# An HGRN2 and forgetting-attention step: a new order at the beginning, in the last recurrent head and in attention's first and last steps

## The chip, the cores and the metric

The kernel runs on one core of a Trainium2 chip, as one program. The metric is the time of one execution on the device in microseconds (us), the median of several; less is better. The engines are TensorE (PE, with PEld for its weight loads), VectorE (DVE), ScalarE (ACT), GpSimd (POOL) and SyncE (SP), whose queue issues most transfers.

## The reference

One inference step of a decoder with two layers, over 512 prompt tokens (one sequence) and 64 sample tokens (eight sequences of eight), model width 1024. In short:

```python
x = concat(x_prompt, x_sample)                 # 576 rows of 1024
h = rmsnorm(x, a_norm) @ a_w_in                # q, forget, value, gate: 8 heads of 128 each
f = lb + (1 - lb) * sigmoid(fz); k = (1 - lb) * sigmoid(-fz)
S_t = diag(f_t) S_(t-1) + k_t v_t^T; o_t = S_t^T q_t       # per head; samples start at state_hgrn
x += (rmsnorm(o, o_g) * silu(gate)) @ a_w_out
x += ffn(x)                                    # SwiGLU, 2816 wide
k, v, logf = shared_kv(x)                      # 16 heads of 64; k normed per head
q = rmsnorm(rmsnorm(x) @ b_wq)
# logit = q.k/8 + cq[t] - ck[s], causal; the samples also see 2048 past rows
# each, read from pages of 128 rows by page_table
x += softmax(logit) @ v @ b_wo
x += ffn(x)
```

Outputs are x, the recurrent states and the new k, v and logf rows.

## The kernel before, in words

Products keep the precision of float32 by splitting both sides into a rounded high part (fp32r) and the rest, the low part: high*high, high*low and low*high are summed, three matmuls for one. So each weight tile (a "unit": 128 output columns) goes SP load, ScalarE high part, GpSimd low part, then 48 matmuls of 128x288 (8 row tiles, 3 products, 2 halves of the 576 tokens). The order of the work is written out by hand for each engine; semaphores join the five lists. There are four blocks with a barrier between them.

*The first block* (`hgrn_layer`) begins with `FirstNorm`: five tiles of tokens (rows 0 to 3 of 128, row 4 of 64) are loaded, squared with a sum (L182), turned to 1/rms by one Ln and one Exp over all (L185 to L189), scaled (L169 on ScalarE, L239 on DVE), transposed by TensorE (L214), and split into xh (L196) and xl (L244). Then come eight heads of four units (q, forget, value, gate; L391). A unit's result is in PSUM banks 0 and 1, and the next unit waits until ScalarE has evicted it (`evicted`). Between the units of head h stand `scores`, `states`, `outputs` and `means` of the heads before. The last head has nothing to stand between: TensorE runs scores(7), means(6), states(7), outputs(7), and the first products of the next block. SP stores the results of head 6 before it fetches head 7's state (`fetch_state`, L343).

*The first trunk* (`trunk`, "t0") is the output product, the feed-forward and the units for q, k and v. Towards its end SP loads the first four cache pages.

*Attention* runs in steps. Steps 0 to 63 (KSTEPS = 64) each transpose two key pages (L1261; `key`), copy them out (L1420, L1551), score them (L1275), and from step 10 on mix two value pages (L1325). Every fourth group adds a decay row through `rowsel` (L1282), which is rounded from `sel`, loaded at the block's start. Eight steps are one sequence: then `exponentials` (a small one of the new rows, L1436, then two halves, L1438), `probabilities` (L1307) and, after the last page, eight matmuls with the new values, `vn` and `ptt` of 8 partitions (L1331). Between, the prompt's own attention is done in 32 pairs of units (L1358 to L1379). Steps 64 to 69 have no keys: they mix four pages each and end the last sequence. PSUM banks 2 to 4 form a ring whose order is that of TensorE's list. After the last step the output weights' first two tiles, loaded by SP behind the pages, get high parts on ScalarE (L1518) and low parts on GpSimd (L1542).

*The second trunk* ("t1") starts by splitting attention's output into parts, tile by tile (`Split`, L1692 and L1697); its first unit waits for each.

```python
for f in range(KD):                      # Split, ScalarE
    act.activation(self.high[:, f, :], self.o[:, f, :], ACT.Copy)
for f in range(KD):                      # Split, DVE
    dve.tensor_tensor(self.low[:, f, :], self.o[:, f, :], self.high[:, f, :], ALU.subtract)
```

## Time and profile before

| | |
|---|---|
| median of three runs | 1877.27 us (1875.54 to 1879.39) |
| the profiled execution's own time | 1880.6 us |
| its span, first to last instruction | 1878.8 us |
| TensorE busy | 1821.9 us, 97% |
| VectorE, ScalarE, GpSimd busy | 49%, 37%, 31% |
| HBM read, written | 254.64 MB, 16.43 MB |
| mean granted TensorE clock | 0.991 of full |

Busy times are sums over the span; matmuls are pipelined and their ends modelled, so a busy TensorE is not one at its peak. The granted clock is a share of 2.4 GHz: 1.00 is that level, 0.50 is 1.2 GHz, and a value between them means that part of the stretch was at either. Idle time of an engine that nothing waits for costs nothing.

### The profile page before, as it was taken

The page shows a single profiled execution, that of the slowest core. Times are in us where ns is not written, and L with a number is a line of the kernel's source. Part 1 is how long each engine was busy: PE and PEld are TensorE (multiplying, and loading weights), DVE is VectorE, ACT ScalarE, POOL GpSimd, SP SyncE. Part 2 cuts the span into 40 slices and gives each one's busy share as a digit, 9 for nine tenths or more (in the row PEclk, how much of TensorE's full clock was granted, in tenths as well). Part 3 has the DMA queues.
Part 4 walks back from the last instruction along what each step waited for, and adds up shares of the span by engine and source line. Part 5 has one row for each costly group of instructions (what it writes and reads, how often), then busy time and mean ns, then how long its engine had stood idle before and what let it go on. Part 6 is the DMA issues. An engine that isn't in the chain of part 4 may idle for free. (4 is left out here: it accounts for less than half of the span.)

```text
span 1878.8 us, 41127 instructions
## 1 busy us (share of the span) xinstructions
PE 1821.9 (97%) x17185; PEld 1693.8 (90%) x17185; DVE 912.5 (49%) x1398; ACT 694.2 (37%) x1089; POOL 579.6 (31%) x295
## 2 busy tenths in 40 slices
PE   6999998999999999999998999999989999999998
PEld 5999997999999999999996677777779999999998
DVE  4767766245555521145653466655543555554000
ACT  5355455432222222245632455555544122122111
POOL 2323331233333343333531011221114334333332
PEclk9999999999999999999999999999989999999999
DMA  5242232232232232242346999999962222223222
GB/s 121 77 111 82 81 100 66 68 90 79 79 90 79 79 94 83 75 141 71 113 138 230 407 379 387 377 355 360 358 223 80 85 85 79 85 84 96 78 77 82
DMA packets 289101, 273.75 MB, mean 146 GB/s; under 512 B 19602, under 2 KB 250099, under 8 KB 288404
## 3 DMA queue, kind: packets, MB, share of 16 engines
q1 hardware_dynamic: 286980, 268.62, 43.8%
q8 instruction: 137, 2.24, 0.5%
q10 hardware_dynamic: 1792, 1.44, 0.3%
q0 software_dynamic: 144, 1.05, 0.1%
q14 instruction: 48, 0.39, 0.1%
HBM read 254.64 MB, written 16.43 MB: 144 GB/s over the span
## 5 line engine op out<-in xcount | busy, mean ns | idle before, releaser
L1973 POOL TENSOR_TENSOR a_wl<-a_wraw,a_wh 128x1024 fp32r<-128x1024 f32 (+2 forms) x91 | 233.3, 2564 | 400.0 <-ACT a_wh L1897 400.0
L1973 POOL TENSOR_TENSOR b_wl<-b_wraw,b_wh 128x1024 fp32r<-128x1024 f32 (+1 forms) x66 | 172.7, 2616 | 297.8 <-ACT b_wh L1897 297.8
L1854 PE MATMUL ps<-xh,a_wh 128*128 128x288 f32 x1104 | 238.4, 298 | 0.0
L1854 PE MATMUL ps<-xl,a_wh 128*128 128x288 f32 x1104 | 237.1, 296 | 0.0
L1854 PE MATMUL ps<-xh,a_wl 128*128 128x288 f32 x1104 | 236.9, 296 | 0.0
L1897 ACT ACTIVATE a_wh<-a_wraw 128x1024 fp32r<-128x1024 f32 (+2 forms) x91 | 100.6, 1105 | 335.0 <-PE ps L1854 315.4
L1897 ACT ACTIVATE b_wh<-b_wraw 128x1024 fp32r<-128x1024 f32 (+1 forms) x66 | 75.0, 1136 | 318.4 <-PE ps L1854 318.4
L1990 DVE TENSOR_TENSOR xT<-xT,ps 128x576 f32<-128x576 f32 x32 | 24.1, 754 | 321.1 <-PE ps L1854 321.1
L1854 PEld LDWEIGHTS ps<-xh,a_wh 128*128 128x128 f32 x1104 | 177.1, 187 | 1.1 <-issue 0.2
L1854 PEld LDWEIGHTS ps<-xh,a_wl 128*128 128x128 f32 x1104 | 177.3, 187 | 0.6
L1854 PEld LDWEIGHTS ps<-xl,a_wh 128*128 128x128 f32 x1104 | 177.2, 187 | 0.6
L1551 DVE COPY at_kt<-ps 128x512 f32<-128x512 f32 x128 | 88.5, 691 | 134.1 <-PE ps L1261 134.1
L1854 PE MATMUL ps<-xh,b_wh 128*128 128x288 f32 x704 | 151.4, 297 | 0.0
L1854 PE MATMUL ps<-xh,b_wl 128*128 128x288 f32 x704 | 151.3, 296 | 0.0
L1854 PE MATMUL ps<-xl,b_wh 128*128 128x288 f32 x704 | 151.1, 296 | 0.0
L631 POOL TENSOR_TENSOR a_wl<-a_wraw,a_wh 128x1024 fp32r<-128x1024 f32 x34 | 82.5, 2430 | 219.9 <-ACT a_wh L526 186.7
L1854 PE MATMUL ps<-f_h,b_wh 128*128 128x288 f32 x608 | 122.1, 300 | 4.7 <-DVE f_h L1697 4.7
L391 PE MATMUL ps<-xh,a_wh 128*128 128x288 f32 x512 | 115.0, 304 | 4.7 <-ACT hg_q L530 1.5
L1854 PE MATMUL ps<-f_h,a_wh 128*128 128x288 f32 x580 | 115.1, 296 | 2.4 <-POOLq L1971 2.4
L1854 PEld LDWEIGHTS ps<-xh,b_wh 128*128 128x128 f32 x704 | 113.8, 189 | 0.1
L1854 PEld LDWEIGHTS ps<-xh,b_wl 128*128 128x128 f32 x704 | 113.7, 189 | 0.0
L1854 PEld LDWEIGHTS ps<-xl,b_wh 128*128 128x128 f32 x704 | 113.7, 189 | 0.0
(352 smaller groups left out, 3879.0 us busy)
## 6 DMA issues: line engine op xcount, KB each, us to landing
a_wraw<-in_w_gate_up SPq DMA_DIRECT2D x44, 512.0 KB, 3.8
b_wraw<-in_w_gate_up SPq DMA_DIRECT2D x44, 512.0 KB, 3.8
xT<-in_cache_k SPq DMA_DIRECT2D x40, 512.0 KB, 6.4
xT<-in_cache_v SPq DMA_DIRECT2D x40, 512.0 KB, 6.9
a_wraw<-in_a_w_in SPq DMA_DIRECT2D x32, 512.0 KB, 4.2
f_h_plain<-in_cache_k SPq DMA_DIRECT2D x30, 512.0 KB, 5.9
xl_plain<-in_cache_v SPq DMA_DIRECT2D x30, 512.0 KB, 6.5
f_h_plain<-in_cache_v SPq DMA_DIRECT2D x30, 512.0 KB, 6.5
```

The lines of the kernel that those rows point to most:

```text
L391: mm = pe.matmul(ps[:, a, 0:HALF], wt[:, n % 2, t, :], at[:, t, a * HALF:(a + 1) * HALF], start=t == 0 and i == 0, stop=t == KD - 1 and i ...
L631: pool.tensor_tensor(wl[:, n % 2], wraw[:, n % 2], wh[:, n % 2].bitcast(F32), ALU.subtract).then_inc(e["low"], 1)
L1551: dve.tensor_copy(kt[:, f, :], ring_bank(x)).then_inc(copied["dve"], 1)
L1854: mm = pe.matmul(ps[0:width(n), bank(n) + a, 0:HALF], wt[:, base(n) + t, 0:width(n)], ap[:, first + t, a * HALF:(a + 1) * HALF], start=kin ...
L1897: act.activation(part(wh, n), part(wraw, n), ACT.Copy).then_inc(e["high"], 1)
L1973: pool.tensor_tensor(part(wl, n), part(wraw, n), part(wh, n).bitcast(F32), ALU.subtract).then_inc(e["low"], 1)
L1990: dve.tensor_tensor(x, x, out(n), ALU.add).then_inc(e["streamed"], 1)
```

## The change

*Beginning.* Each row tile is squared, gets its own Sqrt (ScalarE) and reciprocal (DVE), and is multiplied by both factors in one DVE instruction. ScalarE, DVE and TensorE take the tiles in a new order; tile 4 is transposed inside unit 0. Tiles 1 and 3 share PSUM banks 2 and 3. SP loads the first weights ahead of tile 4 and the second ones ahead of the small late loads; GpSimd forms both parts of these two. Units 1, 3 and 5 write banks 2 and 3, so units up to 5 wait for the eviction before last, and scores(0) for that of unit 5.

*Last head.* fetch_state(7) comes ahead of store(6), means(6) ahead of scores(7), rstd(6) ahead of far_blocks(7).

*Attention.* `sel` is loaded to another place at the end of the first trunk. The small exponential follows the second half. `vn` and `ptt` get 128 partitions, cleared once by GpSimd. From step 64 on, exponentials come ahead of the units' and the copies behind the scores; the last sequence's halves are in two steps. `Split` is gone: ScalarE and DVE form the parts of tiles 0 to 6 in steps 65 to 69, of tile 7 straight from PSUM, and of the samples' columns at the end. The output weights' two tiles get separate high parts; GpSimd makes the first low part, DVE the second.

The diff, cut to its core:

```diff
-    def loads(self, sp):
+    def loads(self, sp, load_weights):
         k = self.k
         sp.dma_start(self.gainrow, k.w["a_norm"]).then_inc(self.gained, 16)
         self.load(sp, 0)
         self.load(sp, 2)
+        load_weights(0)
         self.load(sp, 4)
         for dst, src in k.first_loads:
             sp.dma_start(dst, src, allow_slow_non_contiguous=True).then_inc(self.consts, 16)
+        load_weights(1)
...
+    def square(self, act, c):
         n, _ = self.tokens(c)
-        act.wait_ge(self.weighed, c + 1)
-        act.activation(self.scaled[0:n, c], self.scaled[0:n, c], ACT.Copy, scale=self.mean[0:n, c:c + 1]).then_inc(self.odd, 1)
+        act.wait_ge(self.loaded[c], 16)
+        act.activation(self.junk[0:n, c % 2], self.rows[c][0:n], ACT.Square, accum_out=self.mean[0:n, c:c + 1]).then_inc(self.squared, 1)
+        act.wait_ge(self.squared, c + 1)
+        act.activation(self.mean[0:n, c:c + 1], self.mean[0:n, c:c + 1], ACT.Sqrt, scale=1.0 / D, bias=self.eps[0:n, 0:1]
+                       ).then_inc(self.rooted, 1)
+
+    def round_rows(self, act, c):
+        _, cols = self.tokens(c)
+        act.wait_ge(self.turned, c + 1)
+        act.activation(self.k.xh[:, :, cols], self.banks(c), ACT.Copy).then_inc(self.high, 1)
 
     def scalar(self, act):
-        k, mean = self.k, self.mean
+        k = self.k
         self.load(act, 1)
         self.load(act, 3)
-        act.wait_ge(self.set, 2)
-        act.activation(self.warm, self.warm, ACT.Ln).then_inc(self.warmed, 1)
-        for c in range(5):
-            n, _ = self.tokens(c)
-            act.wait_ge(self.loaded[c], 16)
-            if c >= 2:
-                act.wait_ge(self.squared, c - 1)
-            act.activation(self.junk[0:n, c % 2], self.rows[c][0:n], ACT.Square, accum_out=mean[0:n, c:c + 1]).then_inc(self.squared, 1)
-        act.wait_ge(self.consts, 16 * len(k.first_loads) + 16)
-        act.wait_ge(self.squared, 5)
-        act.activation(mean[:, 0:4], mean[:, 0:4], ACT.Ln, scale=1.0 / D, bias=k.eps[:, 0:1]).then_inc(self.logged, 1)
-        act.activation(mean[0:NS, 4:5], mean[0:NS, 4:5], ACT.Ln, scale=1.0 / D, bias=k.eps[0:NS, 0:1]).then_inc(self.logged, 1)
-        act.wait_ge(self.logged, 2)
-        act.activation(mean[:, 0:4], mean[:, 0:4], ACT.Exp, scale=-0.5).then_inc(self.rooted, 1)
-        act.activation(mean[0:NS, 4:5], mean[0:NS, 4:5], ACT.Exp, scale=-0.5).then_inc(self.rooted, 1)
-        act.wait_ge(self.rooted, 2)
-        self.stretch(act, 1)
-        self.stretch(act, 3)
-        for c in range(5):
-            n, cols = self.tokens(c)
-            act.wait_ge(self.turned, c + 1)
-            act.activation(k.xh[:, :, cols], self.banks(c), ACT.Copy).then_inc(self.high, 1)
+        act.wait_ge(self.set, 3)
+        act.activation(self.warm, self.warm, ACT.Sqrt).then_inc(self.warmed, 1)
+        for c in range(3):
+            self.square(act, c)
+        self.round_rows(act, 0)
+        self.round_rows(act, 1)
+        self.square(act, 3)
+        self.round_rows(act, 2)
+        self.square(act, 4)
+        self.round_rows(act, 3)
+        self.round_rows(act, 4)
...
+        pe.wait_ge(self.identity, 16)
+        for c in range(4):
+            self.turn(pe, c)
+
+    def turn(self, pe, c):
+        k, (n, _) = self.k, self.tokens(c)
+        pe.wait_ge(self.weighed, c + 1)
+        if c >= 3:
+            pe.wait_ge(self.low, c - 1)
+        for f in range(KD):
+            at = f * n
+            mm = pe.transpose(k.ps[:, self.bank(c) + at // 512, at % 512:at % 512 + n], self.scaled[0:n, c, f, :], k.ident[0:n, 0:n])
+        mm.then_inc(self.turned, 1)
...
+        dve.reciprocal(self.mean[0:n, c:c + 1], self.mean[0:n, c:c + 1]).then_inc(self.inverted, 1)
+        dve.wait_ge(self.inverted, c + 1)
+        dve.scalar_tensor_tensor(self.scaled[0:n, c], self.rows[c][0:n], self.mean[0:n, c:c + 1], gains[0:n], ALU.mult, ALU.mult
+                                 ).then_inc(self.weighed, 1)
...
+        for c in range(3):
+            self.weigh(dve, c)
+        self.round_low(dve, 0)
+        self.round_low(dve, 1)
+        self.weigh(dve, 3)
+        self.round_low(dve, 2)
+        self.weigh(dve, 4)
+        self.round_low(dve, 3)
+        self.round_low(dve, 4)
...
+    TWO_BANKS = 5
+    zbank = lambda n: 2 if n <= TWO_BANKS and n % 2 else 0
...
+                fetch_state(H - 1)
                 store(H - 2)
-                fetch_state(H - 1)
...
-                        pe.wait_ge(e["evicted"], n)
+                        pe.wait_ge(e["evicted"], n - 1 if n <= TWO_BANKS else n)
...
+                            if half == (0,) and t == KD // 2:
+                                first.turn(pe, 4)
...
+                    if h == 0:
+                        pe.wait_ge(e["evicted"], TWO_BANKS + 1)
...
+                means(H - 2)
                 scores(H - 1)
-                means(H - 2)
...
+                head_rstd(H - 2)
                 far_blocks(H - 1)
-                head_rstd(H - 2)
...
-                low(0)
-                low(1)
+                for n in range(2):
+                    pool.wait_ge(loaded[n], 16)
+                    pool.tensor_copy(wh[:, n], wraw[:, n]).then_inc(first.rounded, 1)
+                    pool.wait_ge(first.rounded, n + 1)
+                    pool.tensor_tensor(wl[:, n], wraw[:, n], wh[:, n].bitcast(F32), ALU.subtract).then_inc(e["low"], 1)
...
+    def load_rowsel(self, sp):
+        sp.dma_start(self.rowsel, self.k.w["c_rowsel"].rearrange("p a n -> p (a n)")).then_inc(self.selected, 16)
...
-        return SEQ_STEPS * (c + 1) + (half if c < NB - 1 else 0)
+        return SEQ_STEPS * (c + 1) + half
...
-    vn, ptt, headrow = room[0:NQ, 0:D], room[0:NQ, D:D + P], room[0:2 * BH, D + P:D + 2 * P]
+    vn, ptt, headrow = room[:, 0:D], room[:, D:D + P], room[0:2 * BH, D + P:D + 2 * P]
...
+    SPLIT_AT = {KSTEPS + 1: (0, 1), KSTEPS + 2: (2, 3), KSTEPS + 3: (4, 5), KSTEPS + 4: (6,)}
...
-                pe.wait_ge(e["exp"], 3 * c + 2 + g // 2)
+                pe.wait_ge(e["exp"], 3 * c + 1 + g // 2)
...
+                if turned is not None and n >= KSTEPS:
+                    unit_turn(2 * turned)
+                    unit_turn(2 * turned + 1)
...
+                rows = pr[c % 2][:, half * D:(half + 1) * D]
+                act.activation(rows, rows, ACT.Exp, bias=nm[:, 0:1], accum_out=tot[:, half:half + 1]).then_inc(e["exp"], 1)
+                if half == 1:
+                    if c > 0:
                         act.wait_ge(e["filled"], ring["new", c - 1] + 1)
                     act.activation(ptail[:], stail[:], ACT.Exp, bias=nm[:, 0:1], accum_out=tot[:, 2:3]).then_inc(e["exp"], 1)
-                rows = pr[c % 2][:, half * D:(half + 1) * D]
-                act.activation(rows, rows, ACT.Exp, bias=nm[:, 0:1], accum_out=tot[:, half:half + 1]).then_inc(e["exp"], 1)
...
+            def split_high(j):
+                if j == 0:
+                    act.wait_ge(e["filled"], ring["tail", NB - 1] + 1)
+                    act.wait_ge(u["klow"], 2 * KD)
+                    act.wait_ge(u["qlow"], 2 * KD)
+                act.activation(high[:, j, 0:SEQ], o[:, j, 0:SEQ], ACT.Copy).then_inc(split["high"], 1)
+
             def output(j):
                 act.wait_ge(u["mixed"], 4 * j + 4)
+                if j == KD - 1:
+                    act.activation(high[:, j, 0:SEQ], ps[:, OUT_BANK, :], ACT.Copy).then_inc(split["high"], 1)
+                    return
...
+                if n >= KSTEPS:
+                    for half in range(2):
+                        if n == exp_step(NB - 1, half):
+                            exponentials(NB - 1, half)
+                    if turned is not None:
+                        unit_copy(2 * turned)
...
+                if n == KSTEPS + 4:
                     act.wait_ge(nextw["loaded"], 32)
-                    act.activation(k.ring[1][:, 0:2 * KD, :], k.ring[0][:, 0:2 * KD, :], ACT.Copy).then_inc(nextw["high"], 1)
+                    for tile in range(2):
+                        at = slice(tile * KD, (tile + 1) * KD)
+                        act.activation(k.ring[1][:, at, :], k.ring[0][:, at, :], ACT.Copy).then_inc(nextw["high"], 1)
...
+            act.wait_ge(copied["dve"], ordinal["dve"][ring["pick", NB - 1]] + 1)
+            act.activation(high[:, :, SEQ:T], o[:, :, SEQ:T], ACT.Copy).then_inc(split["high"], 1)
...
+            pool.memset(room[:, 0:D + P], 0.0).then_inc(e["cleared"], 1)
...
+            pool.tensor_tensor(wl, wraw, wh.bitcast(F32), ALU.subtract).then_inc(nextw["low"], 1)
...
+            def split_low(j):
+                if j == 0:
+                    dve.wait_ge(u["qhigh"], 4 * KD)
+                    dve.wait_ge(u["qlow"], 2 * KD)
+                dve.wait_ge(split["high"], j + 1)
+                whole = o[:, j, 0:SEQ] if j < KD - 1 else ps[:, OUT_BANK, :]
+                dve.tensor_tensor(low[:, j, 0:SEQ], whole, high[:, j, 0:SEQ].bitcast(F32), ALU.subtract).then_inc(split["low"], 1)
...
+                if n == LAST:
+                    split_low(KD - 1)
+            dve.wait_ge(split["high"], KD + 1)
+            dve.tensor_tensor(low[:, :, SEQ:T], o[:, :, SEQ:T], high[:, :, SEQ:T].bitcast(F32), ALU.subtract).then_inc(split["low"], 1)
+            wraw, wh, wl = (r[:, KD:2 * KD, :] for r in k.ring)
+            dve.wait_ge(nextw["high"], 2)
+            dve.tensor_tensor(wl, wraw, wh.bitcast(F32), ALU.subtract).then_inc(nextw["second"], 1)
...
-                        if split and n == 0:
-                            pe.wait_ge(split.rest, t + 1)
...
-                if split:
-                    split.scalar(act)
...
+            sp.wait_ge(past.spilled, 16)
+            past.load_rowsel(sp)
```

## Rows read from the trace of the kernel before

**Rows 1.** Windows: stretch, length, busy of PE, PEld, DVE, ACT, POOL, clock, DMA share, GB/s.

```profile
0.00:47.00 47.00, 30.39 (x191) 26.81 (x192) 21.84 (x35) 23.87 (x36) 10.47 (x9) 1.00 0.51 121
...
1363.00:1410.00 47.00, 41.08 (x403) 34.09 (x403) 19.02 (x42) 19.87 (x38) 7.28 (x3) 0.85 0.63 216
```

**Rows 2.** The chain of waits: start, us, what; second trunk.

```profile
1389.49 0.69 ACT f_h L1692
...
1391.11 57.64 PE ps L1854 x414
...
1763.32 17.60 PE ps L1854 x132
```

**Rows 3.** Timeline, the beginning: start us, us, engine, line, operation, tiles, count.

```profile
7.33 1.06 ACT L182 ACTIVATE hg_levels<-f_h_plain 128x1024 f32<-128x1024 f32 x1 [3.92 <-DMA f_h_plain<-in_x_prompt]
...
8.74 2.35 DVE L234 TENSOR_TENSOR f_h_plain<-f_h_plain,ps 128x1024 f32<-128x1024 f32 x2 [7.74 <-PE ps L203]
...
14.09 1.28 ACT L188 ACT_TABLE_LOAD   x1
...
16.62 5.59 PE L214 MATMUL ps<-ident,f_h_plain 128*128 128x128 f32 x32 [7.92 <-DVE f_h_plain L239]
...
23.87 0.37 PE L391 MATMUL ps<-xh,a_wh 128*128 128x288 f32 x1 [0.45 <-DVE xl L244]
```

**Rows 4.** Line 214's transposes early and late: duration ns min/median/max.

```profile
L214 PE MATMUL ps<-ident,f_h_plain x9: 421/421/422, 17.5 to 19.2; 128*128 128x128 f32 x9
...
L214 PE MATMUL ps<-ident,f_h_plain x14: 273/273/300, 20.5 to 21.9; 128*128 128x128 f32 x14
```

**Rows 5.** Timeline, ScalarE and GpSimd at attention's end.

```profile
1381.34 1.91 ACT L1518 ACTIVATE b_wh<-b_wraw 128x2048 fp32r<-128x2048 f32 x1 [0.82 <-DMA b_wraw<-in_b_wo]
...
1383.33 4.53 POOL L1542 TENSOR_TENSOR b_wl<-b_wraw,b_wh 128x2048 fp32r<-128x2048 f32 x1 [31.18 <-ACT b_wh L1518]
```

**Rows 6.** The page's groups: busy, mean ns, idle before.

```profile
L391 PE MATMUL ps<-xh,a_wh 128*128 128x288 f32 x512 | 115.0, 304 | 4.7 <-ACT hg_q L530 1.5
```

**Rows 7.** Who waited for whom, TensorE, 24 to 120 us.

```profile
PE ps L391 <- ACT hg_keys L540: 1.3, 1, 1.3
```

**Rows 8.** Timeline, the last head, TensorE and ScalarE.

```profile
323.83 0.75 PE L457 MATMUL ps<-hg_att,hg_vt 128*128 128x128 f32 x4 [3.05 <-DMA hg_s<-in_state_hgrn]
...
329.19 0.60 ACT L574 ACTIVATE hg_pre<-ps 128x512 f32<-128x512 f32 x1 [3.51 <-PE ps L463]
...
340.67 0.60 ACT L269 ACTIVATE xT<-ps 128x512 f32<-128x512 f32 x1 [0.32 <-PE ps L260]
```

**Rows 9.** The tile hg_s: its loads, and their time to landing.

```profile
L343 SPq DMA_DIRECT2D hg_s<-in_state_hgrn x8: 515/527/585, 58.0 to 316.5; - x8
...
DMA to landing us min/median/max: 5.0/5.2/7.2
```

**Rows 10.** Windows of 3 and 2 us.

```profile
324.00:327.00 3.00, 3.00 (x16) 2.77 (x15) 2.96 (x10) 1.67 (x4) 0.00 (x0) 0.55 0.05 16
...
1376.00:1378.00 2.00, 2.00 (x37) 1.56 (x26) 1.29 (x5) 0.97 (x3) 0.00 (x0) 1.00 1.18 302
```

**Rows 11.** Timeline, TensorE in attention's first steps.

```profile
1015.55 0.66 PE L1261 MATMUL ps<-ident,xT 128*128 128x128 f32 x4 [1.90 <-ACT at_kt L1420]
...
1018.60 2.90 PE L1261 MATMUL ps<-ident,f_h_plain 128*128 128x128 f32 x16
```

**Rows 12.** Who waited for whom, TensorE, 1040 to 1360 us: total, times, longest.

```profile
PE ps L1261 <- ACT at_kt L1420: 4.3, 8, 1.6
```

**Rows 13.** Timeline, TensorE around the mixing of values.

```profile
1300.75 0.61 PE L1325 MATMUL ps<-xT,at_pp 128*32 128x256 f32 x8
...
1301.18 0.84 PE L1379 MATMUL ps<-at_upt,f_l_plain 128*32 128x128 f32 x24
...
1321.46 0.63 PE L1331 MATMUL ps<-xl_plain 8*32 8x256 f32 x8
...
1322.03 1.07 PE L1275 MATMUL ps<-at_kt,at_qp 128*32 128x256 f32 x16
```

152 lines of the change are left out of this document (67 added, 85 removed).

## The prediction

> **What bounds the kernel now.** I read the page's shares first: TensorE is busy 97% of the span, every other engine under half. So only stretches in which TensorE stands still, or runs at the lower of its two clocks, can pay. The view by windows, at one 47 us window after another, finds them: 16.6 us of idle TensorE in the first window and 5.9 us around the join of attention and second trunk, there with a granted clock of 0.85 on average [rows 1]; the last HGRN head and attention's first steps are looked at below. The two trunks in between have none. The chain of waits says that the last 488 us are one run of matmuls after the join [rows 2]; nothing in the change makes these fewer, so what is won upstream arrives whole at the end. One step of eight output columns gives the pace: 132 matmuls of 288 columns in 17.60 us [rows 2], 0.133 us each, so a unit of 48 takes 6.4 us at 2.4 GHz.
>
> **The beginning.** Now: the first tile of tokens is there at 7.33; five tiles are squared, then one Ln and one Exp with a table load of 1.28 us between them, then scaled, and only from 16.62 on transposed; the first unit starts at 23.87 [rows 3]. The change makes a pipeline of it. Prices: a square 1.06 [rows 3], with the read of its sum and a root of 128x1 about 1.5 (estimate: the row and two small instructions); a DVE pass over a tile 1.2 (2.35 for two [rows 3]), with the reciprocal 1.4; rounding a tile about 1.0 on ScalarE, 1.2 on DVE; eight transposes 1.7 or 0.9, because they come about 0.21 or 0.11 us apart at the two levels of the clock, 1.2 and 2.4 GHz (estimate from 5.59 us for 32 of both kinds [rows 3] and 421 and 273 ns for one [rows 4]). Walked through the four queues: squares and roots 0 to 2 end at 8.9, 10.4, 11.9; scaled tiles 0 to 2 at 10.3, 11.8, 13.4; transposes 0 to 2 at 12.1, 13.8, 15.5 (slow ones); ScalarE rounds 0 and 1 by 14.9, squares 3 by 16.4, rounds 2 by 17.4; DVE makes low parts 0 and 1 by 16.1, scales 3 by 17.8, and the third low part, on which unit 0 waits, by 19.0. That is 4.8 before 23.87; the fifth tile's transposes now lie inside unit 0 and cost 0.4: 4.4 gained. The weights' high part moves to GpSimd (1.3 for a copy, 2.3 for the subtraction by half of [rows 5]); both loads are queued earlier, the first by one row tile, and the parts are there at about 16 and 20, when unit 0 wants the first at 19 and unit 1 the second at 26. On SP's queue the sample rows' load slips behind 512 KB: they are wanted at 17.4, so free.
>
> Units 1 to 5 change banks: each no longer waits for the eviction of the one before. These waits are 4.7 us [rows 6], of which 0.4 is for a low part at unit 0's start; leaves 4.2. What is late next is GpSimd's low part for unit 3, behind the forget gate's four activations: about 6.5 us after unit 1 ends, when TensorE wants it 6.4 after: 0.1. Against that, head 0's scores must now wait until unit 5 is evicted, as unit 2 did before: 1.3 [rows 7]; behind it stands TensorE's whole queue. Net 2.8. Beginning: **7.2**, bounds 4 and 8.7.
>
> **The last head.** TensorE waits 3.05 us, until 323.83, for the state of the last head [rows 8]; its load is issued at 316.5 and takes 7.2 us, the other seven at least 5.0 and in the middle 5.2 [rows 9]. After that long stand the granted clock is 0.55, the lower level of 1.2 GHz for most of the window [rows 10], and the outputs, the means, a chain of Ln, Exp and gates end at 340.67 + 0.60 [rows 8]. The change issues the load ahead of two stores and puts means(6) ahead of scores(7), so that rstd(6) runs before far_blocks. The scores start some 0.7 later; the load is then issued at about 316.3 and lands at 321.5; blocks are placed and states ready by 321.7. So 2.1 from the load. TensorE's longest stand is then about 1 us, so I take the full clock: outputs last 3.05 instead of 5.4 (323.83 to 329.19 [rows 8]): 2.3. The two table loads of rstd(6) (2.6 us) move before the attended blocks, under DVE's work; the means after next_unit's first two tiles come 1.6 earlier against the squares. Together **6.0**; bounds 2.1 (the load alone) and 6.5.
>
> **Attention's first steps.** ScalarE waits for the row selector's load, and so a key copy is late: TensorE stands 1.90 us, and then 16 transposes take 2.90 us [rows 11] where the pitch of 0.11 gives 1.8. The selector now comes at the end of the first trunk, one more DMA on SP behind the spill and ahead of four pages; nothing on SP waits there for TensorE soon. The stand goes (1.9, or 1.0 if pages 4 and 5 are next to be late: they land just about when wanted), the slow transposes too: **2.9**, bounds 1 and 3.6. GpSimd's clearing of 1152 columns comes before it waits anyway.
>
> **In the steps.** The small exponential of each sequence moves behind the second half, so the first half, and the key copy behind it, are earlier. Waits for that copy are 4.3 us in eight, the longest 1.6 of another cause [rows 12]: at most 2.7; I take **1.3**. Padding the new values from 8 to 128 partitions keeps TensorE in one shape: eight matmuls take 0.57 (1321.46 to 1322.03) against 0.43 of full height (1300.75 to 1301.18) [rows 13], so 0.14, and at most as much again on entering: eight times, 1.1 to 2.2; I take **1.7**. The selector of the first probabilities (one semaphore step lower) is met long before.
>
> The Trainium skill (TensorEngine Tiling (Array Packing), section Tiling Modes) says that changing the tiling mode drains TensorE. By it the entry and the exit both cost here, which is the upper bound, 2.2, and the sum would be 0.5 more.
>
> **The last steps and the join.** Exponentials and scores come before the copies, so TensorE no longer stands around 1363. But the DMA engines are full then (share 1.18 at 1376 [rows 10]), so the last pages and the output weights land when they did: at 1381.34 ScalarE gets the weights [rows 5]. This is what is late next, and caps the gain. From there, now: 1.91 for the high part, 4.53 on GpSimd, end 1387.86 [rows 5], barrier until 1389.49, and TensorE only at 1391.11 after the split's first tile [rows 2]. After: 1.05 for one half, 2.3 on GpSimd, to 1384.8; ScalarE second half, last tile's and samples' high parts to 1384.6; DVE their low parts and 1.25 for the weights' second half, to 1386.6. So 1.2 earlier, and TensorE starts 1.7 after that, without the split: 1388.3. **2.8**, bounds 1.6 (only the split) and 6. The split tiles 0 to 6 lie in steps in which ScalarE and DVE are half idle.
>
> **Sum.** 7.2 + 6.0 + 2.9 + 1.3 + 1.7 + 2.8 = 21.9 off 1880.6 of the profiled execution (span 1878.8) is 1858.7; the median of the runs is 3.3 lower, so **1855.4**.
>
> **Rivals.** *The clock falls all the same*: TensorE still has gaps of 1 us in the last head and attention, and the beginning is slow throughout. Then 3.4, 1.1 and 1.4 are missing: 1861. For it: two tiles of transposes were slow at 16.6 although the page grants 1.00. *Memory bounds attention*: the DMA share is near 1 in the whole stage, so what is won inside (5.9) would end in waits for pages: 1861. Against it: no row of TensorE's waits names a page. *The tail gives all*: the weights land earlier with the earlier pages: 1852. *Table switches*: if Square and Sqrt do not share a table, ten loads of 1.28 [rows 3] stand in ScalarE's queue, eight ahead of unit 0: 10.3 to 12.8, 1867. Against it: Square ran after Ln with no load between. The Trainium skill (ScalarE: Activation LUTs, section What ACT_TABLE_LOAD costs) adds a drain and makes a switch 2.66 us: ten would be 26.6, and the kernel 4.7 slower. Its section Table sets has Ln and Exp in one set; the row disagrees, a load stands between them. *Slower*: a faster TensorE in attention's steps runs onto pages that are not there, each stand lowers the clock, and the steps run at half of it. Each microsecond so spent costs half; from 44 us on it eats the 21.9; 60 us would give 1885.
>
> **How the numbers follow.** Forecast 0.58; clock 0.18; memory 0.09; tail 0.08; tables 0.04; slower 0.03. All lower bounds together give 1867, all upper 1848; **1849 to 1866** leaves out tables, slower and corners of the rest. A measurement tells 0.2% (3.8 us): faster 0.95, same 0.02, slower 0.03.
>
> **What would show it.** First matmul of unit 0 near 19.0, with no ScalarE table load between squares and roots; no stand over 0.3 in units 1 to 4 and one of 1.3 ahead of the first scores; the state's load lands near 321.5 (less 7) and the windows there grant 1.00; no stand for the key copy at attention's second step; TensorE's first matmul of the second trunk right behind the barrier. Wrong if unit 0 starts after 21, if the clock reads 0.5 in the last head, or if the output weights' GpSimd part ends later than 3.5 us after they land.

## The result, and the profile after

The changed kernel takes **1867.93 us** (median of five runs, 1867.41 to 1869.82), the kernel before 1878.47 beside it (1875.54 to 1879.83): a ratio of **0.9944**, 95% interval 0.9933 to 0.9954. That is 10.5 us faster, where 21.9 were forecast; 1855.4 was 12.5 too low, and the range ended 2 below the measured time. The profiled execution's span is 1866.1 against 1878.8: 12.7 less, and this difference is the one that the two traces can split.

| stretch (us in the span) | before | after | gain | forecast | after, again (e16) |
|---|---|---|---|---|---|
| start to the unit behind the first scores (unit 6) | 71.87 | 66.65 | 5.2 | 7.2 | 5.6 |
| to the last raw transpose ahead of scores(7) | 236.92 | 237.10 | -0.2 | 0 | -1.7 |
| from there to the first trunk (the last head) | 34.23 | 30.61 | 3.6 | 6.0 | 3.2 |
| the first trunk | 664.14 | 664.32 | -0.2 | 0 | -2.4 |
| attention's start to its 193rd key transpose | 54.60 | 55.54 | -0.9 | 2.9 | 2.3 |
| to the 961st (the steps) | 276.33 | 273.60 | 2.7 | 1.3 + 1.7 | 2.7 |
| to the second trunk (last steps and join) | 53.02 | 50.94 | 2.1 | 2.8 | 2.4 |
| the second trunk | 487.69 | 487.37 | 0.3 | 0 | 1.7 |
| sum | 1878.80 | 1866.13 | 12.7 | 21.9 | 13.8 |

The last column is the same changed kernel run once more. It differs from the first by up to 3.2 us in a stretch, and the sum by 1.1, so a single row is to be trusted to a few microseconds at most where the clock moves, and better where it doesn't. So I compare medians of runs where a whole kernel is judged, and stretches where both traces show the same clock.

The mean granted clock is 0.991 in both traces. That is the first thing that the forecast had otherwise: it counted on less half clock in two of the places. By windows of the kernel after (stretch, length, busy of PE, PEld, DVE, ACT and POOL, clock, DMA share, GB/s):

```profile
18.00:21.00 3.00, 2.83 (x13) 2.83 (x14) 2.58 (x4) 1.67 (x4) 1.09 (x1) 0.50 0.25 37
...
315.00:318.00 3.00, 2.92 (x12) 2.04 (x11) 2.49 (x10) 2.61 (x7) 0.00 (x0) 0.50 0.55 166
318.00:321.00 3.00, 3.00 (x15) 2.78 (x15) 2.86 (x8) 0.11 (x1) 0.00 (x0) 0.50 0.31 86
...
1007.00:1009.00 2.00, 0.51 (x3) 0.54 (x4) 0.00 (x0) 0.00 (x0) 1.82 (x4) 0.62 1.00 395
1009.00:1012.00 3.00, 3.00 (x15) 2.74 (x13) 0.69 (x1) 1.20 (x2) 1.74 (x2) 0.50 1.01 326
...
1046.00:1049.00 3.00, 3.00 (x33) 1.38 (x26) 0.78 (x3) 0.00 (x0) 0.00 (x0) 0.59 1.03 406
1376.00:1379.00 3.00, 0.24 (x1) 0.24 (x2) 1.11 (x1) 0.00 (x0) 0.00 (x0) 0.52 0.00 0
1379.00:1382.00 3.00, 3.00 (x13) 3.00 (x14) 0.00 (x0) 0.00 (x0) 0.00 (x0) 0.50 0.73 237
```

At 1.2 GHz (0.50) now: the first matmuls of the kernel, the last head's states and outputs, attention's third step, and the join. Before, the last head (0.55 [rows 10]) and the join (0.85 on average [rows 1]) had half clock, too. The stands in front of these places are seen on TensorE's timeline of the kernel after:

```profile
18.17 1.97 PE L217 MATMUL ps<-ident,f_h_plain 128*128 128x128 f32 x8 [3.04 <-DVE f_h_plain L233]
19.79 0.59 PE L403 MATMUL ps<-xh,a_wh 128*128 128x288 f32 x1
...
61.41 0.30 PE L424 MATMUL ps<-ident,hg_v 128*128 128x128 f32 x1 [1.37 <-ACT hg_keys L556]
...
65.33 0.35 PE L408 MATMUL ps<-hg_levels 128*32 128x32 f32 x18 [1.18 <-issue]
...
304.60 1.21 PE L487 MATMUL ps<-hg_rs,mean 128*128 128x288 f32 x4 [0.58 <-DVE f_h_plain L795]
...
310.77 0.52 PE L408 MATMUL ps<-hg_levels 128*32 128x32 f32 x20 [1.60 <-issue]
...
312.94 1.13 PE L459 MATMUL ps<-hg_vt,hg_kt 128*128 128x128 f32 x8 [1.58 <-POOL hg_vm L656]
...
317.55 1.19 PE L471 MATMUL ps<-hg_att,hg_vt 128*128 128x128 f32 x4
...
1008.49 3.65 PE L1288 MATMUL ps<-ident,f_h_plain 128*128 128x128 f32 x16 [2.39 <-issue]
```

Unit 0 starts at 19.79 (before 23.87 [rows 3]). Line 471, ahead of which TensorE had waited 3.05 for the state [rows 8], has no wait. Ahead of the third step's transposes is a new stand of 2.39. Two things were in no step of mine: the 1.18 and 1.60 inside the scores, put down to "issue" (the engine waits for nothing that the profile shows), and the 1.58 ahead of the states, which waits for GpSimd's mask. For the last head both could be read in the kernel before, where the means stand between scores and states (TensorE's timeline, before):

```profile
315.02 0.46 PE L396 MATMUL ps<-hg_levels 128*32 128x64 f32 x14 [1.66 <-issue]
315.51 1.24 PE L473 MATMUL ps<-hg_rs,mean 128*128 128x288 f32 x4
317.14 1.13 PE L445 MATMUL ps<-hg_vt,hg_kt 128*128 128x128 f32 x8 [0.39 <-POOL hg_vm L640]
```

A stand of 1.66 was there already, and the wait for the mask was 0.39 only because the means ran ahead of it.

The join, all engines (the kernel after; timeline):

```profile
1370.74 2.00 ACT L1571 ACTIVATE b_wh<-b_wraw 128x1024 fp32r<-128x1024 f32 x2 [1.71 <-DMA b_wraw<-in_b_wo]
...
1371.51 0.63 PE L1367 MATMUL ps<-at_pickq,at_om 128*128 128x32 f32 x4
1371.87 2.35 POOL L1599 TENSOR_TENSOR b_wl<-b_wraw,b_wh 128x1024 fp32r<-128x1024 f32 x1 [29.97 <-ACT b_wh L1571]
...
1372.32 2.45 DVE L1706 TENSOR_TENSOR f_h<-xh_plain,f_h 128x512 fp32r<-128x512 f32 x1
...
1374.69 0.68 DVE L1706 TENSOR_TENSOR f_h<-ps,f_h 128x512 fp32r<-128x512 f32 x1
1375.30 0.68 DVE L1755 TENSOR_TENSOR f_h<-xh_plain,f_h 128x512 fp32r<-128x512 f32 x1
1375.89 1.21 DVE L1758 TENSOR_TENSOR b_wl<-b_wraw,b_wh 128x1024 fp32r<-128x1024 f32 x1
...
1378.76 1.33 PE L1913 MATMUL ps<-f_h,b_wh 128*128 128x288 f32 x4 [6.62 <-POOLq L2028]
```

ScalarE gets the weights at 1370.74, 10.6 earlier than before [rows 5], but 10.3 of that is the shift of the whole kernel: counted from the 961st key transpose it is 42.9 us now and was 43.3. By the same count TensorE is done with attention 4.0 earlier (last pick at 43.7 against 47.7), and its stand ahead of the second trunk grows from 4.68 to 6.62. The row names the barrier. What comes last ahead of it is DVE, which ends at 1377.10, 1.66 before TensorE starts (1.65 or 1.66 in every trace that has this join). DVE's 128x512 subtraction takes 2.45 us and the next two of the same size 0.68.

The chain of waits is as it was, one run of matmuls behind the join, with the same 17.60 a step as in [rows 2]:

```profile
1805.09 17.60 PE ps L1913 x132
...
1859.83 0.66 PE ps L1927 x4
```

### The profile page after: what moved, and what is told of

Read it like the earlier page. It is cut to its first block and busy times, and to the rows that moved or that the text cites. A ratio compares the mean times of both kernels' runs of the same rounds, so it can differ in the third digit from the quotient of the medians.

```text
span 1866.1 us, 41137 instructions
## 1 busy us (share of the span) xinstructions
PE 1816.4 (97%) x17185; PEld 1692.5 (91%) x17185; DVE 915.1 (49%) x1401; ACT 693.0 (37%) x1089; POOL 581.0 (31%) x298
## 5 line engine op out<-in xcount | busy, mean ns | idle before, releaser
L647 POOL TENSOR_TENSOR a_wl<-a_wraw,a_wh 128x1024 fp32r<-128x1024 f32 x32 | 78.0, 2439 | 199.4 <-ACT a_wh L542 184.3
```

The source lines that it names most:

```text
L647: pool.tensor_tensor(wl[:, n % 2], wraw[:, n % 2], wh[:, n % 2].bitcast(F32), ALU.subtract).then_inc(e["low"], 1)
```

## The experiments

Four theories were open. **Clock:** the gain is eaten by stretches at 1.2 GHz behind stands that are still there. **Order:** a part of the new order costs by itself (the means ahead of the scores). **Instructions:** TensorE starves for instructions inside the scores, a loss that comes and goes with their place in the list. **Memory:** pages bound attention's first steps. Unless said otherwise, an edit is made to the changed kernel. The 95% intervals reach 2 to 3 us to each side, so medians that differ by less than that from the changed kernel's are not told from it by themselves; the stretch in which an edit works says more.

**e1: the beginning alone.** The kernel before with the diff's hunks of `FirstNorm`, the banks and the first weights, nothing else.

> The kernel before with the new beginning alone (row pipeline, weights' high part on GpSimd, five units in two pairs of banks); last head, attention and join as before. Read so far from the trace after: unit 0 starts 4.1 us earlier, the first scores 6.4, and 1.2 are given back in a stand inside those scores, so 5.2 at the unit behind them. Theory 'the gain of each stage stays': the kernel is 5.0 to 5.5 us faster than before, with the last head starting 5.0 earlier and everything behind it shifted by the same. Rival 'the clock takes it back': the half-clock stretches behind (in the last head, at attention's start, at the join) fall elsewhere and total gain is anywhere from 2 to 8, with the trunk's start off by more than 1 from 5.0.

Measured: 1872.88, ratio 0.9969 (0.9958 to 0.998): 5.7 us, of it 5.1 at the unit behind the first scores in the trace. More than half of the whole gain is the beginning. What the trace also shows: the last head, with its old order, takes 30.1 here and not 34.2, with a wait of 2.11 for the state (TensorE's timeline of e1):

```profile
319.47 0.68 PE L471 MATMUL ps<-hg_att,hg_vt 128*128 128x128 f32 x4 [2.11 <-DMA hg_s<-in_state_hgrn]
```

Of the 10.2 us at half clock that stood there before [rows 10] 3.4 are left: my sum had taken a clock loss for a property of the order. The new order takes 30.6 to 32.1 there, with 6.8 to 10.2 us at half clock, in nine traces whose last head is the changed kernel's, so by this one trace of e1 the two moves in the last head gained nothing together.

**e2: the means behind the scores again**, with rstd(6) behind the attended blocks; the state's fetch stays ahead.

```diff
-                means(H - 2)
                 scores(H - 1)
+                means(H - 2)
```

> The changed kernel with one part undone: the means of head 6 stand behind the last head's scores again, and the two table loads of its root behind the far blocks. The state's load stays ahead of the stores. In the trace after, the means cost 1.0 ahead of the scores, and GpSimd's masking of the samples' values and all behind come 1.0 later. Theory 'the order of the means brings little of itself (my forecast gave it 1.6 at the end of the chain)': scores 1.0 earlier, outputs of the last head within 0.5 of the trace after, the first trunk starts 0 to 1.5 later than 334.4. Rival 'the table loads on the path': the two loads (2.6 us) stand ahead of the raw copies again, and the trunk starts 2 to 3 later.

Measured: 1864.85, ratio 0.9932 (0.9918 to 0.9945), 3.1 us faster than the changed kernel. TensorE's timeline of e2:

```profile
310.90 0.46 PE L408 MATMUL ps<-hg_levels 128*32 128x64 f32 x14 [1.79 <-issue]
...
311.38 1.24 PE L487 MATMUL ps<-hg_rs,mean 128*128 128x288 f32 x4
313.02 1.13 PE L459 MATMUL ps<-hg_vt,hg_kt 128*128 128x128 f32 x8 [0.40 <-POOL hg_vm L656]
...
317.77 0.68 PE L471 MATMUL ps<-hg_att,hg_vt 128*128 128x128 f32 x4 [1.10 <-DVE hg_S L787]
```

The means' 1.24 us stand where the changed kernel waits 1.58 for the mask; the wait is 0.40. The states keep the full clock, and the last head takes 28.7 against 30.6 (28.7 in e12 and e13, too, where the means are not ahead of the scores either). The order costs 1.9 or more in its own stretch, and in my sum it had the wrong sign. Of the 3.1 between the medians the rest is not located: the two intervals overlap.

**e3: the fetch late again**, behind the stores of head 6; the means stay ahead.

```diff
-                fetch_state(H - 1)
                 store(H - 2)
+                fetch_state(H - 1)
```

> The changed kernel with one part undone: the last head's state is fetched behind the two stores of head 6 again. Issue 1.0 later and in competition with 512 KB of store. In the trace after, the state is issued at 311.4 and TensorE asks for it at 317.5, so it has 6.1 us; the late one needs 1.0 and 7.2. Theory 'the load decides': TensorE stands 2.1 more, outputs at 319.7, the half clock longer (10.2 instead of 6.8), 2.1 to 4 slower at the trunk's start. Rival 'the load is hidden anyway behind the chain of DVE': no change within 0.5.

Measured: 1870.81, ratio 0.9952 (0.9939 to 0.9966), 2.9 slower than the changed kernel, with overlapping intervals. TensorE waits 1.11 for the state; the last head takes 35.3, with 17 us of it at half clock. The early fetch is worth 1.1 by its wait here, 2.1 by e1's, and some 3 as medians go.

**e4: one pair of banks for all units.**

```diff
-    TWO_BANKS = 5
+    TWO_BANKS = 0
```

> The changed kernel with one part undone: units 1 to 5 use one pair of banks and wait for the eviction of the one before. The waits before were 4.2 us in five; what two pairs cost in their place was 1.4 ahead of the first scores and, if it hangs on that wait, the stand of 1.2 inside the scores. Theory 'the stand inside the scores is the price of the wait ahead of them (the queue of instructions had run dry)': it is gone here, and the kernel is 1.5 to 1.8 slower than the changed one at the unit behind the scores. Rival 'it belongs to the place in the code': the stand of 1.2 stays, 2.8 slower there.

Measured: 1870.96, ratio 0.9959 (0.9945 to 0.9973), 3.0 slower. From unit 0 to unit 6 50.39 us against 46.86, though the new stand inside scores(0) is gone with the wait ahead of them. Some of the 3.5 is clock: with as much half clock behind unit 0 as here the two pairs take 47.8 (e7, e8, e13, e17), so the second pair is worth 2.6, forecast 2.8.

**e5: stands filled.** Transposes of the identity into a free bank keep TensorE busy: 24 ahead of tile 3, 13 ahead of states(7), 6 at the end of that block, 40 behind attention's last step.

```diff
+            if c == 3:
+                pe.wait_ge(self.low, 1)
+                for _ in range(24):
+                    pe.transpose(k.ps[:, 0, 0:P], k.ident[:], k.ident[:])
```

> The changed kernel with transposes of the identity into free PSUM banks where TensorE otherwise stands: 24 ahead of the fourth row tile, 13 between the last head's scores and states, 6 at the end of that block, 40 at the end of attention. They compute nothing that is read. In the trace after, TensorE stands 3.0, 1.6, 2.2 and 6.6 us there, and the half clock (6.8 us in the last head, 3.4 at the first trunk's start, 6.8 at the join) begins inside or just behind them. Theory 'the stands bring the half clock': the granted clock is 1.00 in the last head and behind the join, the outputs of the last head take 3.6 instead of 4.9, the second trunk has made up 2.1 more by its 400th matmul; 3 to 6 us faster than the changed kernel. Rival 'the half clock comes whatever TensorE does': the same total of about 27 us at half clock, no gain, and up to 1 lost where the filling overlaps real work.

Measured: 1875.77, ratio 0.9991 (0.9981 to 1.0001): the whole gain is gone. Every head's scores now have a stand, 13.5 us in eight. So the 24 were tried alone.

**e9: only the 24 transposes ahead of tile 3.**

> The changed kernel with one of the four fillings of the run with filled stands alone: the 24 transposes ahead of the fourth row tile. They lie in a stand of 3.0 us, so in time they cost nothing; what they do besides is to shift all later instructions of TensorE by 48 matmul and weight-load instructions. In the run with all four fillings TensorE stood 13.5 us in eight stands inside the eight heads' scores, with no semaphore to wait for, one each, where the changed kernel has three of 3.1 together. Theory 'the scores, some 700 short instructions in 3.5 us, outrun the loading of instructions, and whether they do hangs on where a loaded piece ends, so on the count of instructions ahead': the eight stands are here too, 10 us lost between the first scores and the last head. Rival 'the stands came from the fillings in the last head or at its end, or from chance': three stands as in the changed kernel.

Measured: 1878.9, ratio 1.0003 (0.9994 to 1.0013). Who waited for whom on TensorE, 50 to 345 us, in e9:

```profile
engine line waited for: us in total, times, longest us
PE ps L412 <- issue: 13.9, 8, 2.0
PE ps L463 <- POOL hg_vm L660: 1.6, 1, 1.6
```

The changed kernel has 3.1 us of this in three. The 24 lie in a stand of 3.04, before unit 0, and cost nothing there; the only thing that they are seen to do further back is to move each later instruction of TensorE's by 48 (each transpose is a weight load and a matmul). The theory of the instructions holds. In the scores TensorE issues 500 instructions in 3.9 us (250 matmuls and their weight loads; the 700 in 3.5 us of my expectation was a miscount); the page's third part names a queue that loads instructions, and it moves little and in large pieces (the kernel after):

```profile
q8 instruction: 137, 2.24, 0.5%
```

That is 16 KB a packet, and with 35,095 instructions of TensorE in the trace 256 a packet. From one head's scores to the next head's the trace has 1,023 instructions and four packets, so every head meets the packets at the same place in its list, which fits that 48 more hit all eight. In the changed kernel's heads 1, 2, 3, 5 and 6 a packet starts 0.1 to 0.3 us behind the scores' first instruction and the next 3.4 to 3.6 us later, and there is no stand. In e9's heads 0 to 6 the first of the two starts 2.4 to 4.7 us ahead of the scores, the next 3.0 to 3.5 us into them, and TensorE stands from 3.9 on. In the last head of every kernel, of the one before too, a packet starts 2.6 to 3.4 us into the scores, as in e9, and there is a stand each time. That the packet's place in the list decides it follows from e9 and e5; what sets the time at which a packet is asked for is not shown. Nor is the place all: the changed kernel's second trace (e16), with the same list, has 4.6 us in six stands, not 3.1 in three.

**e10: the other three fillings (13, 6 and 40), without the 24.**

> The changed kernel with the other three fillings alone: 13 transposes between the last head's scores and states, 6 at the end of that block, 40 at the end of attention. Nothing ahead of any head's scores is shifted, so the scores should stand as in the changed kernel. Theory 'the stands bring the half clock': no half clock between 312 and 345 and none behind the join, 3 to 5 us faster than the changed kernel. Theory 'only a part of it': the stretches get shorter (3.4 instead of 6.8) but one still follows the block's end and the join, whose barriers no filling covers, 0 to 2 faster. Rival 'it comes whatever TensorE does': as in the changed kernel within 0.5 in every stage.

Measured: 1866.1, ratio 0.9931 (0.9913 to 0.9949), 1.8 faster. Windows of e10:

```profile
315.00:318.00 3.00, 2.99 (x24) 2.29 (x22) 3.00 (x8) 2.95 (x4) 1.03 (x1) 1.00 0.69 196
318.00:321.00 3.00, 1.68 (x13) 1.02 (x10) 2.50 (x11) 2.82 (x7) 0.00 (x0) 1.00 0.62 181
...
1379.00:1382.00 3.00, 3.00 (x13) 3.00 (x14) 0.00 (x0) 0.00 (x0) 0.00 (x0) 0.50 0.73 214
```

The last head is at full clock throughout (29.3 us against 30.6), so there the clock theory holds; it is no guarantee, for e5 has 3.4 us of half clock in the middle of the same head with the same filling. Behind the join the clock falls all the same, for 3.4 us and not 6.8: the 40 transposes end 2.6 us before the second trunk starts. With the same 40 and 2.0 us left, e15's clock does not fall there, and e17's does.

**e13: the means inside the scores**, ahead of their third column block.

```diff
+                        if h == H - 1 and a == 2:
+                            means(h - 1)
```

> The changed kernel with the means of head 6 neither ahead of nor behind the last head's scores, but in their middle, ahead of the third of the four blocks of rows. They are four matmuls of 288 columns, 1.04 us of work that needs few instructions, at the place where TensorE stands 1.6 us with no semaphore to wait for. Theory 'that stand is the loading of instructions': the loading goes on under the means, the stand shrinks by about 1.0 and the time from the scores' first transpose to the states is 1.0 shorter than with the means behind them. Rival 'the stand is something else (the clock, a hidden wait)': it stays at 1.6, and the sum from the raw turns to the outputs is as in the changed kernel.

Measured: 1865.87, ratio 0.9937 (0.9923 to 0.995). TensorE's timeline of e13:

```profile
311.12 0.52 PE L408 MATMUL ps<-hg_levels 128*32 128x32 f32 x20 [0.44 <-issue]
...
313.29 1.13 PE L461 MATMUL ps<-hg_vt,hg_kt 128*128 128x128 f32 x8 [1.58 <-POOL hg_vm L657]
```

The stand inside shrinks from 1.60 to 0.44 once four long matmuls give the loading time (0.29 in e15 with the same edit, 1.6 to 2.3 in all traces without it), which supports the theory of the instructions. But the wait for the mask is 1.58 again: the time is the same as with the means behind. There is one wait to fill, and either will do.

**e6: the page numbers read early**, ahead of attention's barrier, so that SP issues pages 4 and 5 sooner.

```diff
+            self.pages.ahead = {l: self.pages.number(sp, l) for l in (Pages.EARLY, Pages.EARLY + 1)}
```

> The changed kernel, but SyncE reads the numbers of pages 4 and 5 from the page table at the end of the first trunk, not in attention; their loads are then issued about 1.7 and 2 us earlier than 1001.1 and 1002.8 (trace after). Theory 'attention's third step now waits for page 5': TensorE's stand of 2.39 ahead of that step's transposes shrinks by 1.7 to 2.4, and the 6.8 us of half clock at 1007.5 with it or in part; 2 to 4 us faster at the 65th key transpose. Rival 'the DMA engines are full there': the pages land when they did, and the stand stays over 1.5.

Measured: 1866.46, ratio 0.9936 (0.9923 to 0.9948). Pages are issued 1.1 us behind the row's load and no longer 2.6, yet the third step starts 9.54 behind attention's start and not 9.81, no gain beside the 9.5 to 9.95 of the traces without this edit. So issue wasn't the limit: the DMA share is 1.00 there (windows above). From attention's start to its 65th key transpose it is 16.85, against 19.25 in the changed kernel's first trace, but that is the clock: 17.00 in e16, the unedited kernel, with no half clock there.

**e14: a store of 1 MB moved behind these pages**, with e6's edit.

> The changed kernel with page numbers 4 and 5 read early and, besides, the last store of the prompt's key rows (1 MB, issued 1.3 us ahead of attention's first load) moved behind the loads of pages 4 and 5. Reading the numbers early alone brought the loads 1.5 us forward and TensorE only 0.3. Theory 'the DMA engines are full with the row stores': without 1 MB ahead of them (2.6 us at 390 GB/s) the pages land over 1.5 earlier, the stand in the third step is under 0.5, and attention's start to the third step takes 7.5 to 8.3 instead of 9.5 to 9.8. Rival 'a page takes as long as it takes there': the stand stays over 1.

Measured: 1866.87, ratio 0.994 (0.9927 to 0.9954). TensorE's timeline of e14:

```profile
1010.87 2.08 PE L1292 MATMUL ps<-ident,f_h_plain 128*128 128x128 f32 x16
...
1015.64 0.30 PE L1292 MATMUL ps<-ident,f_h_plain 128*128 128x128 f32 x1 [1.17 <-issue]
```

The stand ahead of the third step is gone (8.27 behind the start), and one of 1.17 ahead of the fourth has come; the 65th transpose is where it was (16.79). The memory theory holds in part: the first four steps end when the pages allow.

**e7: both weight tiles' low parts on DVE**, none on GpSimd.

```diff
-            pool.tensor_tensor(wl, wraw, wh.bitcast(F32), ALU.subtract).then_inc(nextw["low"], 1)
+            for tile in range(2):
+                wraw, wh, wl = (r[:, tile * KD:(tile + 1) * KD, :] for r in k.ring)
+                dve.wait_ge(nextw["high"], tile + 1)
+                dve.tensor_tensor(wl, wraw, wh.bitcast(F32), ALU.subtract).then_inc(nextw["second"], 1)
```

> The changed kernel, but both halves of the output weights' low part are formed by VectorE at the end of attention, none by GpSimd. In the trace after, a subtraction of 128x512 on VectorE takes 2.45 us while GpSimd works on its half, and 0.64 else; VectorE ends last, 1377.1. Theory 'VectorE is held up by GpSimd': the 2.45 becomes 0.64, one half of 1.21 is added: VectorE ends 0.6 earlier after TensorE's last matmul and the second trunk starts 5.9 to 6.2 behind that matmul instead of 6.6. Rival 'VectorE's own work is the bound': it starts 0.6 to 1.2 later (7.2 to 7.8 behind).

Measured: 1867.02, ratio 0.9942 (0.993 to 0.9955). Timeline of e7:

```profile
1372.28 0.68 DVE L1704 TENSOR_TENSOR f_h<-xh_plain,f_h 128x512 fp32r<-128x512 f32 x1
...
1374.08 2.35 DVE L1757 TENSOR_TENSOR b_wl<-b_wraw,b_wh 128x1024 fp32r<-128x1024 f32 x2
...
1378.08 1.33 PE L1912 MATMUL ps<-f_h,b_wh 128*128 128x288 f32 x4 [5.98 <-POOLq L2027]
```

With GpSimd quiet the same subtraction takes 0.68. TensorE starts 0.64 earlier behind its last pick, but only 0.3 of that is this edit's: from the moment at which ScalarE takes the weights it is 7.76 here (7.73 in e12, e15 and e17, which have this edit) and 8.02 to 8.05 in twelve traces with a half on GpSimd; the rest is the weights' arrival. Two subtractions of 128x1024 on DVE (2.35) take as long as one on GpSimd.

**e8: the old order of the last steps**; copies first, the exponentials of the last sequence in one step, the parts still formed there.

> The changed kernel with the last steps' order undone (copies and transposes of the pairs ahead of the last sequence's exponentials again); the forming of the high and low parts in those steps stays. From the traces before and after: between the last key transposes and the last new-probability transpose the change won 4.8, of which 3.4 is a half-clock stretch of 6.8 us that is gone; behind it 2.7 are lost in the join (TensorE's stand there 6.6 instead of 4.7, and less of a start). Theory 'the order won 4.8, the join gave 2.4 back': here the last new-probability transpose is 3 to 5 later, the second trunk starts 2.5 to 5 later. Rival 'the join's end is set by the weights' load and VectorE': the second trunk starts within 1 of the changed kernel's time.

Measured: 1867.01, ratio 0.9938 (0.9925 to 0.9951), no slower than the changed kernel. The 961st key transpose to the second trunk is 50.63 against 50.94. The last transpose of new probabilities comes 1.6 later, and nothing at the end does: the order of the last steps is worth nothing, because the end hangs on the weights. ScalarE takes them 42.5 to 43.7 us behind the 961st key transpose in every trace, before's and e1's included. The old code there in e1 took 52.70, and 1.7 of the difference lies behind the weights (9.74 from them to the second trunk, 8.02 here): the parts formed early, without `Split`, and the weights in two halves. No run separates these two.

**e11: the new values' matmuls on 8 partitions again.**

```diff
-                        mm = pe.matmul(out, ptt[:, tile(t)], pairs(vn, t), start=False, stop=True, skip_group_check=True)
+                        mm = pe.matmul(out, ptt[0:NQ, tile(t)], pairs(vn[0:NQ], t), start=False, stop=True, skip_group_check=True)
```

> The changed kernel with the new values' matmuls on 8 rows again, not on 128. My forecast gave the padding 1.7 (1.1 to 2.2) over eight sequences; the waits for key copies went from 2.0 to 0.8 in the trace after, so 1.5 of the 2.7 gained in the steps is left for it. Theory 'the change of shape costs on entry and exit': 1.1 to 1.7 later from the 193rd to the last key transpose. Rival 'the padding brings nothing and the steps gained by something else': within 0.3.

Measured: 1869.83, ratio 0.9954 (0.9937 to 0.9971), 1.9 slower as runs go. From the 193rd to the 961st key transpose 275.08 against 273.60 (273.6 to 273.8 in all other traces of the changed kernel and its edits): 1.5 for padding (forecast 1.7). The other part, the small exponential, is read from who waited for whom over the steps, in the kernel after:

```profile
PE ps L1288 <- ACT at_kt L1451: 0.8, 2, 0.5
```

Before it was 2.0 in six over the same steps (the 4.3 of [rows 12] also held two ahead of the 193rd key transpose): 1.2 gained, 1.3 forecast.

**e12: e2, e6 and e7 together.**

> The three edits that were not slower put together: means of head 6 behind the last head's scores, page numbers 4 and 5 read early, both weight low parts on VectorE. From the medians of their own runs: 3.1, 1.5 and 0.9 under the changed kernel; where these are real they add up to 1862 or 1863. Rival 'they are the scatter of the half clock from run to run': 1865 to 1867, only the 0.6 of VectorE at the join sure.

Measured: 1862.62, ratio **0.9917** (0.9903 to 0.9932), the best median: 15.2 under the kernel before beside it, and its interval lies below the changed kernel's. It is not told from e2's. The traced execution was the slowest of the five (1867.54), so its stretches are not the median's.

**e15: e13, e14, e7 and e10's fillings together.**

> The changed kernel with the means inside the last head's scores, page numbers early, the store behind the pages, both weight low parts on VectorE, and the late fillings (13, 6 and 40 transposes). From the single runs: 1.0 at most for the means, 1.5 to 2 for the pages, 0.6 for VectorE, 1 to 3 for the half clock in the last head and at the join; 1861 to 1864 if they add up. Rival 'the half clock moves elsewhere': 1864 to 1867.

Measured: 1863.3, ratio 0.9919 (0.9905 to 0.9932), not told from e12.

**e16: the changed kernel once more**, no edit, for the scatter of one kernel's trace.

> The changed kernel itself once more, beside the others, for the scatter. Theory 'the half clock's place differs from execution to execution and is worth 2 to 3 us': the stages ahead of the first half-clock stretch take what they took, to 0.3; the half clock begins at other places than 314.6, 335.1, 1007.5 and 1045.0, and from attention's start to the 193rd key transpose it takes 51.8 to 52.4, not 55.5. Rival 'it is fixed for a kernel': the same places and 55.5 again.

Measured: 1867.63, ratio 0.9945 (0.9932 to 0.9959). Windows of e16, at attention's third step:

```profile
1012.00:1015.00 3.00, 2.58 (x24) 1.90 (x24) 1.38 (x2) 1.20 (x2) 2.47 (x3) 1.00 1.04 354
```

TensorE's timeline of e16:

```profile
1012.28 1.97 PE L1288 MATMUL ps<-ident,f_h_plain 128*128 128x128 f32 x16 [2.38 <-issue]
```

The same 16 transposes, behind the same stand: 1.97 us at full clock here, 3.65 at 0.50 in the first trace. In turn the first trunk's start had twice as much half clock here, 6.8 us.

**e17: e2, e14, e7 and of the fillings the 6 and the 40.**

> The changed kernel with the means of head 6 behind the last head's scores again, page numbers early and the store behind the pages, both weight low parts on VectorE, and the two late fillings (6 transposes at the end of the HGRN block, 40 at the end of attention). From the profiles so far: from the last of the four raw turns to the first trunk 28.7 (changed kernel 30.6 to 32.1), second trunk 6.2 behind attention's last matmuls (changed kernel 6.9), with the half clock of the join short or gone. Theory 'these stages' gains are real': 1861 to 1864, 4 to 6 under the changed kernel. Rival 'the half clock falls elsewhere': 1864 to 1867.

Measured: 1864.53, ratio 0.9929 (0.9916 to 0.9943), no better than e12. Its scores have 4.5 us of "issue" in five stands; nothing in it stands ahead of the first seven heads' scores, and e16 has as much, so this is scatter and not the edit.

## Why the prediction was off, by its steps

**The mechanisms of the beginning were right, with 2.0 missing of 7.2.** Unit 0 started at 19.8, not 19.0: the first matmuls ran at 1.2 GHz behind the 3.04 stand (19.2 in e4, e5 and e9, where the clock is full until then). No table load stood between squares and roots, units 1 to 4 have no stand, and the scores waited 1.37 (forecast 1.3). What failed is the price of "head 0's scores must now wait until unit 5 is evicted": behind this wait came a second one of 1.18 for instructions, which no row of mine priced. e4, without the wait, is without the second stand. Together 0.8 + 1.2 are the missing 2.0.

**The last head is the step that failed most by reasoning.** "TensorE's longest stand is then about 1 us, so I take the full clock" was wrong: 1.60 and 1.58 follow each other (310.77 and 312.94), and the clock was at half from 315 on; the outputs took 5.0 us and not 3.05. The first of the two stood in the kernel before, too (1.66 at 315.02), and I had not read it. The means ahead of the scores, forecast as +1.6 through the table loads and squares, cost 1.9 in this stretch (e2; 3.1 as medians go), because they had filled the wait for the mask. The load's own part, forecast 2.1, is what e1 with the late fetch still waits (2.11); in e3 it is 1.11. And the base was off: 34.2 before, with 10.2 us at half clock, was 30.1 in e1 with 3.4.

**Attention's first steps: 2.9 became -0.9 in the first trace and 2.3 in e16.** The 55.5 of the first trace is the exception: it is 52.0 to 53.6 in nine other traces with this code there, against 54.6 before and 54.4 in e1, so 1 to 2.6 are gained. The key copy's stand went, the pages' came (2.39 where I had allowed 1.0 in the lower bound), and half clock decides the rest: before's trace had 6.8 us of it at the start (1007.0 to 1010.4, 1017.2 to 1020.6), the first one after 10.2 (1007.5 to 1014.3, 1045.0 to 1048.4, behind a stand of 1.92 for a key copy), e16 none. That "no row of TensorE's waits names a page" spoke against the memory rival was a weak argument: the stand that pages caused is put down to "issue".

**The steps were right** in both parts (1.2 of 1.3, 1.5 of 1.7), and the trace gives 2.7 for the 3.0.

**The last steps and the join: 2.1 of 2.8.** "The last pages and the output weights land when they did", the cap, held, counted from the steps' end: 42.9 us against 43.3. What was mis-sized is the way from the weights to the second trunk: 9.8 before, 7.0 forecast, 8.02 measured. The forecast had DVE done 5.3 behind the weights, and it was done 6.4 behind, held up by GpSimd beside it; TensorE's start 1.7 after that was right. It had 2.3 for GpSimd (2.35 measured) and DVE's part at its usual price. e13 is the counter-check: there DVE's first subtraction began 0.3 ahead of GpSimd's and took 0.68, and the way was 7.05. The Trainium skill (GPSIMD Engine Reference, section Specifications) says that GpSimd shares its SBUF interfaces with VectorE and contends with its instructions that have two SBUF inputs. This subtraction is one, and the trace agrees: 2.45 beside GpSimd and 0.68 alone (e7).

**The rivals.** The clock rival described what happened: the granted clock is 0.991 as before, and its 1861 was still too low, since it gave the other steps in full. Of memory a part came true, at attention's start (e14) and in the weights' arrival at its end. The steps did not end in waits for pages, and neither tables nor tail came.

**The sum.** Of the 9.2 between 21.9 and 12.7: 2.0 at the beginning (1.2 of it instructions), 2.4 in the last head, 3.8 at attention's start (3.2 of it is that one execution's, by e16), 0.3 in the steps, 0.7 in the join, and nothing in the trunks. That nothing hides a term which the forecast had at none: 3.4 us of half clock at the first trunk's start. Without it that trunk takes 664.1 to 664.3 (before, e10), with 3 to 6 us of it 665.1 to 666.6, so 1 to 2.4 more, in every other trace but the first of the kernel after, where a faster stretch (last section) made up for it. By e16 the missing 8.1 divide otherwise: 1.6 at the beginning, 1.7 in the heads behind it (the "issue" stands above all), 2.8 in the last head, 2.4 in the first trunk, 0.6, 0.3 and 0.4 in attention and the join, and 1.7 come back in the second trunk. As medians go the gain is 10.5 and not 12.7: the traced execution of the kernel before took 1880.6, 2.1 above its median, that of the kernel after was its median. My base had that in it: before's own trace had 10.2 us of half clock in the last head, e1's, with the same code there, 3.4.

## What to carry to other kernels

Before an operation is moved ahead, look what it fills where it stands: the means hid a wait for GpSimd, and ahead of the scores they hid nothing. Do not tie a half clock to the place where one trace has it: run the unchanged kernel twice before a trace's slow stretch is put into a sum. When a few more instructions in an idle stretch make a kernel slower far behind it, read the "issue" stands inside bursts of short matmuls first.
